# Two norms by halves of the tokens, later turns in an attention, and a short convolution in two parts, in a hybrid block with a two-layer mixer behind it

## Reference

```
def rms_norm_2(x, g):
    return x * rsqrt(mean(x * x, -1) + EPS) * g
for l in range(2):
    hx = modulate(rms_norm_2(x, norm1_g[l]), mod_x[0], mod_x[1])
    x = x + mod_x[2] * token_mixers(...)          # conv of 31 taps, differential attention, spatial gating, 3-tap conv, then @ w_out
    x = x + mod_x[5] * (square(relu(modulate(rms_norm_2(x, norm2_g[l]), mod_x[3], mod_x[4]) @ w1[l])) @ w2[l])
return rms_norm_2(x, final_g)

# first layer's attention, one head, one block of 128 queries
s = where(valid, q @ k.T * Dh**-0.5, NEG);  p = exp(s - max(s));  o = (p @ v) / sum(p)
# 3-tap convolution of the mixer
y_d = bg * depthwise_conv(cg * xin, conv_d_w)
```

## Time and profile before

| | |
|---|---|
| Runs | 2136.23, 2140.30, 2147.45 us; median 2140.3 |
| Profiled execution | 2144.59 us, its span 2142.8 us, 26206 instructions |
| Busy share of the span | TensorE matmul 96%, weight load 81%, VectorE 59%, ScalarE 37%, GpSimd 4% |
| Mean granted clock of TensorE | 0.990 of full speed |
| HBM | read 232.53 MB, written 12.06 MB |

### The profile page before, as it was taken

The page is one execution under the profiler, slowest core; times in us unless marked ns, Lnnn a source line. Parts: engine busy times, 40 slices in busy tenths (PEclk is TensorE's granted clock), DMA queues, the critical chain, the costliest instruction groups (busy, mean ns, idle before and its releaser), DMA issues.

```text
span 2142.8 us, 26206 instructions
## 1 busy us (share of the span) xinstructions
PE 2050.4 (96%) x11020; PEld 1740.1 (81%) x11020; DVE 1267.6 (59%) x1674; ACT 792.9 (37%) x1107; POOL 75.1 (4%) x83
## 2 busy tenths in 40 slices
PE   6999999999999999899999999999998899999998
PEld 5978877878788988788888888888787787888886
DVE  6466765766756886736546456464689645343343
ACT  4333334495253355524212122122536634232231
POOL 0000000000030000021000000001100010000001
PEclk9999999999999999999999999999999999999999
DMA  8543432523422531213323233232353122222221
GB/s 288 219 149 127 177 118 93 196 91 121 194 84 94 165 99 50 69 59 120 109 98 118 92 127 116 99 119 89 128 165 89 70 89 79 98 99 99 98 97 61
DMA packets 53077, 249.17 MB, mean 116 GB/s; under 512 B 6272, under 2 KB 10512, under 8 KB 34528
## 3 DMA queue, kind: packets, MB, share of 16 engines
q1 hardware_dynamic: 51072, 242.41, 32.8%
q10 hardware_dynamic: 1296, 2.63, 0.3%
q0 software_dynamic: 592, 2.46, 0.3%
HBM read 232.53 MB, written 12.06 MB: 114 GB/s over the span
## 4 chain that ended last, share of the span: by engine, by line
PE 82%; DVE 10%; ACT 3%; issue 3%; DMA 1%; POOL 0%; ACTq 0%; DVEq 0%; SPq 0%; POOLq 0%
PE banks L1805 68%; DVE small L1313 2%; ACT whi_f L1955 1%; DVE wlo_f L2146 1%; PE banks L631 1%; DMA mvr<-in_mst 1%; PE banks L622 1%; PE banks L1828 1%; PE banks L1830 1%; PE banks L1829 1%; PE banks L511 1%; DVE ntx L2180 1%; PE banks L586 1%; PE banks L585 1%; PE banks L587 1%
## 5 line engine op out<-in xcount | busy, mean ns | idle before, releaser
L1805 PE MATMUL banks<-hxh,whi_f 128*128 128x512 f32 x1440 | 583.9, 405 | 23.6 <-ACT hxh L1966 10.0
L1805 PE MATMUL banks<-hxh,wlo_f 128*128 128x512 f32 x1440 | 568.3, 395 | 0.0
L1805 PE MATMUL banks<-hxl,whi_f 128*128 128x512 f32 x1440 | 554.1, 393 | 0.0
L2146 DVE TENSOR_TENSOR wlo_f<-raw_f,whi_f 128x2048 fp32r<-128x2048 f32 x133 | 305.0, 2293 | 184.9 <-ACT whi_f L1955 184.8
L1955 ACT ACTIVATE whi_f<-raw_f 128x2048 fp32r<-128x2048 f32 x133 | 253.7, 1908 | 309.1 <-PE banks L1805 290.9
L1805 PEld LDWEIGHTS banks<-hxh,whi_f 128*128 128x128 f32 x1440 | 273.2, 190 | 87.0 <-issue 28.4
L1805 PEld LDWEIGHTS banks<-hxh,wlo_f 128*128 128x128 f32 x1440 | 272.9, 190 | 60.3
L1805 PEld LDWEIGHTS banks<-hxl,whi_f 128*128 128x128 f32 x1440 | 272.5, 189 | 58.7 <-issue 1.9
L1457 DVE SCALAR_TENSOR_TENSOR xT<-banks,small,xT 128x512 f32<-128x512 f32 x80 | 59.5, 750 | 253.2 <-PE banks L1805 253.2
L1805 PE MATMUL banks<-fxh,whi_f 128*128 128x512 f32 x512 | 202.8, 396 | 2.2 <-DVE cT L1457 1.1
L1805 PE MATMUL banks<-fxh,wlo_f 128*128 128x512 f32 x512 | 201.0, 393 | 0.0
(11 more groups left out here) (329 smaller groups left out, 3127.8 us busy)
## 6 DMA issues: line engine op xcount, KB each, us to landing
raw_f<-in_wst SPq DMA_DIRECT2D x133, 1024.0 KB, 4.8
mvr<-in_mst SPq DMA_DIRECT2D x120, 512.0 KB, 5.7
stack<-qk_parts SPq DMA_DIRECT2D x36, 192.0 KB, 6.7
x_kept<-xT SPq DMA_DIRECT2D x2, 2048.0 KB, 8.5
raw_f<-in_wst SPq DMA_DIRECT2D x8, 384.0 KB, 5.9
xT<-x_kept SPq DMA_DIRECT2D x2, 1536.0 KB, 8.7
qk_parts<-qk_h SPq DMA_DIRECT2D x3, 768.0 KB, 3.8
qk_parts<-qk_l SPq DMA_DIRECT2D x3, 768.0 KB, 3.6
```

Source lines behind the costliest of these rows:

```text
L1805: last = pe.matmul(o, (wh, wl)[w][:, k, c, :], r[part][:, k, :], start=(k == order[0] and parts is not LOW and (w, part) == (0, 0)), stop= ...
L2146: dve.tensor_tensor(wlo[r][:], raw[r][:], whi[n % 2 if n > N_FIRST else n][:].bitcast(F32), ALU.subtract).then_inc(w_lo, 1)
```

## The change

First attention: turned and values move from 9 and 12 steps behind the scores to 11 and 15. Short convolution: its six operations are put behind the maxima of two consecutive units, three and three; the low part of the first output chunk and `sub_norm(0)` come one unit later each. Layer 1's last output chunk and its last feed-forward chunk are multiplied by halves h of the tokens (256 columns each): both c of the first half, then both of the second, with sums, root, inverse and spread of the first half's norm inside the second. The first feed-forward chunk behind it takes pieces: four tiles of the first half, four tiles of the second half, then four whole tiles. The final products and the stores go by halves too, in five stores instead of eight. Cut to its core (the list of semaphore counts and the ScalarE and VectorE halves of the same steps are left out):

```diff
 def unit_turned(u):
-    return unit_scores(u) + 9
+    return unit_scores(u) + 11
 
 
 def unit_values(u):
-    return unit_scores(u) + 12
+    return unit_scores(u) + 15
...
+PIECES = [(h, k) for h in range(2) for k in range(4)] + [(None, k) for k in range(4, KT)]
+def columns(h):
+    return slice(0, T) if h is None else slice(TH * h, TH * h + TH)
...
-                gemm(n, 1, own)
-                norm_sums(SX, n_ff[l], nsq2)
-                norm_spread(SX, n_ff[l])
-                gemm(n + 1, 0, own, ready=(lambda k: wait_high(SX, n_ff[l], k), lambda k: wait_low(SX, n_ff[l], k)))
+                half_gemm(n, hxh, hxl, n_ff[1], nsq2)
+                piece_gemm(n + 1, n_ff[1], nsq2)
...
+                        if l and n == base + N_FF - 1:
+                            half_gemm(n, fxh, fxl, n_fin, nsqf)
+                            half_sums(n_fin, nsqf, 1)
+                            half_spread(n_fin, 1)
+                            continue
...
-            norm_root(SX, n_ff[l])
-            for k in range(KT):
-                norm_high(SX, n_ff[l], hxh, k, mod_shift(1, k, 0))
+                    half_square(n_ff[1], nsq2, c, 0, n)
+                half_root(n_ff[1], 0)
+                half_square(n_ff[1], nsq2, 0, 1, n)
+                for i, (_, k) in enumerate(PIECES):
+                    if i == 2:
+                        half_square(n_ff[1], nsq2, 1, 1, n)
+                    if i == 4:
+                        half_root(n_ff[1], 1)
+                    piece_high(n_ff[1], i, mod_shift(1, k, 0))
             split(n + 2)
...
-            run(p.cut, p.units, late={p.cut: short_conv, p.cut + 1: lambda: split(base + N_WIN),
-                                         p.cut + 2: lambda: sub_norm(0)})
+            run(p.cut, p.units, late={p.cut: lambda: short_conv(0), p.cut + 1: lambda: short_conv(1),
+                                         p.cut + 2: lambda: split(base + N_WIN), p.cut + 3: lambda: sub_norm(0)})
...
             else:
+                q = n_ff[1]
                 for c in range(2):
-                    last_x(c)
-            norm_inverse(SX, n_ff[l])
-            modulate(SX, n_ff[l], xT, hxh, hxl, 1, 0)
+                    half_residual(q, n, 0, c, 0)
+                half_inverse(q, 0)
+                half_residual(q, n, 0, 0, 1)
+                for i in range(len(PIECES) + 1):
+                    if i == 2:
+                        half_residual(q, n, 0, 1, 1)
+                    if i == 4:
+                        piece_low(q, 3)
+                        half_inverse(q, 1)
+                    if i < len(PIECES):
+                        piece_scale(q, i)
+                    if i > 0 and i != 4:
+                        piece_low(q, i - 1)
             split(n + 2)
...
+                    if end and not two and i == 3:
+                        for c in range(2):
+                            half_residual(n_fin, n, 1, c, 0)
+                        half_inverse(n_fin, 0)
+                        half_residual(n_fin, n, 1, 0, 1)
+                        continue
...
+            def final(k, h):
+                x_ = xT[:, k, columns(h)]
+                dve.scalar_tensor_tensor(x_, x_, vcol("final_g", k, 1), aux[:, 1 + h, 0:TH], ALU.mult, ALU.mult
+                                         ).then_inc(x_done, 1)
+            dve.wait_ge(SX.spread, half_count(n_fin, 0))
+            for k in range(KT):
+                if k == 5:
+                    half_residual(n_fin, base + N_FF - 1, 1, 1, 1)
+                final(k, 0)
+            half_inverse(n_fin, 1)
+            dve.wait_ge(SX.spread, half_count(n_fin, 1))
+            for k in range(KT):
+                final(k, 1)
...
-            for k in range(KT):
-                sync.wait_ge(x_done, KT + k + 1)
-                sync.dma_start(out[:, k, :], xT[:, k, :]).then_inc(stored, 16)
-            sync.wait_ge(stored, 16 * KT)
+            stores = [(0, 0, 4), (0, 4, 8), (1, 0, 4), (1, 4, 6), (1, 6, 8)]
+            for h, k0, k1 in stores:
+                sync.wait_ge(x_done, KT * (1 + h) + k1)
+                sync.dma_start(out[:, k0:k1, columns(h)], xT[:, k0:k1, columns(h)]).then_inc(stored, 16)
...
+            def half_sums(q, sq, h):
+                if h:
+                    pe.wait_ge(SX.rooted, half_count(q, 0))
+                else:
+                    pe.wait_ge(SX.added, q.a + KT - 3)
+                for i, slot in enumerate((0, KT - 2, KT - 1)):
+                    if i:
+                        pe.wait_ge(SX.squared, q.s + KT - 2 + 2 * h + i)
+                    for j in (2 * h, 2 * h + 1):
+                        last = pe.matmul(SX.st[:, j:j + 1], sq[:, slot, j * P:(j + 1) * P], ones[:, 0:1],
+                                         start=(i == 0 and j == 2 * h), stop=(i == 2), skip_group_check=True)
+                last.then_inc(SX.summed, 1)
+            def half_spread(q, h):
+                pe.wait_ge(SX.inverted, half_count(q, h))
+                for j in range(2):
+                    last = pe.matmul(aux[:, 1 + h, j * P:(j + 1) * P], SX.rs[:, 2 * h + j:2 * h + j + 1].to_broadcast([P, P]),
+                                     ident, start=True, stop=True)
+                last.then_inc(SX.spread, 1)
+            def half_gemm(n, hi, lo, q, sq):
+                weights(n)
+                for h in range(2):
+                    r = [(hi[:, :, columns(h)], lo[:, :, columns(h)])]
+                    for c in range(2):
+                        if h == 0:
+                            pe.wait_ge(acc_free[c], n)
+                        for k in range(KT):
+                            if (h, c, k) == (1, 0, 4):
+                                half_sums(q, sq, 0)
+                            if (h, c, k) == (1, 1, 1):
+                                half_spread(q, 0)
+                            last = step(n, n % 2, k, c, r, at=lambda r: acc[:, c, T * h:T * h + TH])
+                        last.then_inc(acc_ready[c] if h else x_part, 1)
+            def piece_gemm(n, q, sq):
+                weights(n)
+                for i, (h, k) in enumerate(PIECES):
+                    if i == 2:
+                        half_sums(q, sq, 1)
+                    if i == 4:
+                        half_spread(q, 1)
+                    r = [(hxh[:, :, columns(h)], hxl[:, :, columns(h)])]
+                    wait_high(SX, q, i)
+                    for c, parts in ((0, HIGH), (1, HIGH), (0, LOW), (1, LOW)) if k < KT - 1 else \
+                            ((0, HIGH), (0, LOW), (1, HIGH), (1, LOW)):
+                        if i == 0 and parts is HIGH:
+                            pe.wait_ge(acc_free[c], n)
+                        if c == 0 and parts is LOW:
+                            wait_low(SX, q, i)
+                        last = step(n, n % 2, k, c, r, (0 if i == 0 else -1, KT - 1),
+                                    lambda r: acc[:, c, columns(h)], parts, True)
+                        if k == KT - 1 and parts is LOW:
+                            last.then_inc(acc_ready[c], 1)
```

153 lines of the change are left out of this document (109 added, 44 removed).

## The result

The changed kernel took 2117.36 us (median of 4 runs, 2115.37 to 2123.61), the kernel before in the same comparison 2141.52 (4 runs): ratio 0.9891, 95% interval 0.9857 to 0.9926. The forecast was 2116.5. A second comparison of the same kernel (experiment 10) gave 2120.13 against 2144.69, 0.9881 (0.9859 to 0.9904). The medians differ by 24.2 and 24.6 us, 1.1 to 1.2%.

What follows compares the result with a forecast made beforehand. TensorE, 82% of the chain, was taken as the bound, with the gain in its waits and half-clock stretches. Terms -11.5 - 1.7 - 6.8 - 1.8 - 2.1 = -23.9 us from the median 2140.3 gave 2116.5, range 2108 to 2127.

Steps and rivals of the forecast that it cites:

- First attention, -11.5 and -1.7: First attention: TensorE's waits for turn and values go from 15.1 to 3.6 us; a half-clock stretch near 343 ends.
- one step more before the values, so 1.76 - 0.69 = 1.07: First attention: the fifth unit's copy moves behind a chunk end, leaving TensorE a new 1.07 us wait before the values.
- Convolution, -6.8: Second block's attentions: splitting the convolution shortens TensorE's turn waits in both layers and ends half clock behind them, -6.8 us.
- Layer 1's 1.4: Layer 1's convolution: of 2.0 us moved away only 1.4 counts, since the combination must await its own exponentials.
- without a wait over 0.5: Expected sign: the turns at 876.7 and 1706.2 us, behind the convolution, come without a wait over 0.5 us.
- Layer 0's 2.6: Layer 0's convolution: moving three operations a unit later takes 2.6 us from TensorE's 2.86 us wait.
- The join, -1.8: Chunk before layer 1's second norm, by halves: chunk 2.1 us longer, next-but-one chunk starts 17.0 behind its end; -1.8 us.
- The end, -2.1: Final chunk, norm and products by halves: chunk 2.1 us longer, then 6.4 instead of 10.6 to the last product; -2.1 us.
- (1): Rival: first attention's waits move instead of ending, as later copies fall behind chunk ends; half the gain lost, 2123; chance 0.17.
- (2): Rival: join by halves is no gain, TensorE's idle before late weight halves brings 1.2 GHz; 2122 to 2125.5; chance 0.15.
- (3): Rival: the split convolution brings no more than its later place costs, +6.8 us, 2123; chance 0.05.
- (4): Rival, slower: weight loads bind in the 240 new narrow matmuls, each 0.19 us more, +45.6, 2162; chance 0.02.

Runs made afterwards that it cites:

- experiment 10: The changed kernel unedited, measured again in a second comparison with the kernel before: 2120.13 us against 2144.69, ratio 0.9881.
- experiment 9: Changed kernel with scaled output ahead of the next exponential, weights' high part earlier, high-part products first, later steps for first attention's last waits: 2109.76 us, ratio 0.9833.
- Experiments 7, 8 and 12: On the changed kernel: 7 moves the weights' high part before the join's fifth piece (join 51.76 us); 8 multiplies high-part products first (2112.23 us); 12 both (2115.06 us).
- experiment 6: Changed kernel with last chunk, final norm and stores whole again, the join still by halves: 2124.27 us, one run.
- experiment 1: Kernel before with only the first attention's steps changed (9 and 12 become 11 and 15): 2127.71 us against 2145.78, ratio 0.992.
- experiment 3: Kernel before with only the three-tap convolution split in two parts: layer 1's stretch from gating's sums to transposes 50.00 us.
- experiment 2: Kernel before with only the first attention's values moved to 15 steps, the turn left at 9: first attention's stretch 339.7 us, 9.4 less than before.

## Why the prediction was right, and where its steps were not

**The total** came out at 2117.4 for 2116.5 (by its own sum, 2140.3 - 23.9, it is 2116.4). That it came so close is luck: the first attention was undersized by 4.2, and the others were oversized by 2.7 together by the table, by 4.1 by the means given above. The lower end of the range, 2108, isn't what it is said to be: the bounds of attention and convolution together give 2110.6.

**First attention, -11.5 and -1.7: right in place, too small.** Measured 17.4. Two steps failed. First, "one step more before the values, so 1.76 - 0.69 = 1.07": I counted what the new order puts between scores and turn (the values of the unit before), not what it puts between a copy and its values, which is the next unit's scores. For the fifth unit these are the sixth's, from 167.5 to 168.7; so its wait vanished, and the thirteenth's was 0.65 instead of 1.8. The last unit's, forecast 0.7, was 0.91. Left 1.6 instead of 3.6: 2.0 of the 4.2. Second, a wait was priced at its idle time in the trace. Removing two waits of 0.91 and 0.65 in experiment 9 shortened the stretch by 1.8 to 1.9, some 0.15 more for each; ten waits fewer and one stretch at half clock (13.5 + 1.6) gave 17.4, 0.2 more for each. The turn behind a wait is itself recorded longer (0.87 to 0.88 us, mostly 0.82 without one). The Trainium skill's Perfetto Trace Analysis (Tensor Engine Instruction) says that TensorE's end time is estimated from the instruction's size, "a model, not a measurement"; the difference agrees in sign with idle that is read from such ends, but no run here shows that this is its cause.

**Convolution, -6.8: right in kind.** Measured 3.1 and 2.7. Layer 1's 1.4 is what the executions without half clock show. It leaves 0.8 of the 2.19 us wait, and 0.79 is what the turn at 1680.42 waits; the sign "without a wait over 0.5" contradicted the sum, and fell. Layer 0's 2.6, for which no row was given, was 1.5 to 2.1: the turn a unit later, at 859.06, now waits 0.55 us, a remainder that I took as none. The half clock at the wait was there in layer 0 in all three profiles with the convolution whole and ScalarE's order as before, in layer 1 in two of the three. So 1.4 for each was right in size (1.6 in layer 0, 1.3 in layer 1) and not certain in layer 1.

**The join, -1.8: mechanism right, size wrong.** All its events came: the chunk 2.4 us longer (forecast 2.1), the idle at the fifth piece, ScalarE's and then VectorE's weight half last, 17.5 behind the chunk's end (17.0). The failed terms are small ones of one sign. Sums and spread took 1.24 + 0.44 where 1.55 stood; the narrow matmuls took 0.121; VectorE's second run of pieces began 5.1 instead of 4.7 behind the chunk and its last low part ended 14.1 behind it, 0.9 later than I had added up; ScalarE's weight half began 13.2 behind it where 12.6 stood. The formula that the prediction sets beside its rows is given by the Trainium skill's TensorE page (TensorE: Matmul & The Clock Gate, Back-to-back issue gap) for an isolated matmul, and not for a stream with weight loads; the measured 0.121 us decides. Experiments 7, 8 and 12 show what the late weight half costs: 1.9 us of the join, more than the halves gain in any execution. The prediction had this wait in its sum.

What the sum did not see is that the join before has no one length: 6.8 or 10.2 us of half clock, by execution. Against the shorter one the halves bring nothing. So even the 0.9 is that of a profile with the longer stretch.

**The end, -2.1: 1.3.** The last chunk +2.4; from its end to the last product 6.1 us (forecast 6.4) instead of 10.5; but the tail to the end of the span, "taken as it is", grew from 2.7 to 3.4. That is the step that failed: the last store lands later, a median of 3.0 us behind its issue instead of 2.2 for the same 256 KB, and with the old stores (experiment 6) the tail is 2.65 again. The new stores have rows of 1 KB instead of 2 KB and stand behind stores of 512 KB; no run tells which of the two counts.

**The rivals.** (1) fell with experiment 1. (2) was half right: no gain at the join in some executions, but by the late weights, not by the clock. TensorE stands idle there 1.11 and 2.07 us, and the granted clock stayed 1.00 through it in all eight executions with the join by halves. It fell to 0.50 in all six with the join whole. In the kernel before it fell at 1770.3, behind 2.4 us in which TensorE did no more than sums (stretch, us, busy by engine, PEclk):

```profile
1767.90:1770.30 2.40, 1.68 (x15) 1.59 (x14) 0.72 (x1) 0.63 (x1) 0.00 (x0) 1.00 0.63 154
1770.40:1774.70 4.30, 2.08 (x8) 1.79 (x9) 1.67 (x4) 1.11 (x3) 0.00 (x0) 0.50 0.35 149
```

The Trainium skill's TensorE page (TensorE: Matmul & The Clock Gate, Part 1) says that idleness throttles the array. The join whole agrees with it; the two idles of the join by halves, 1.11 and 2.07 us, did not bring it about, so the rival that the rule favoured was the wrong one. (3) fell with experiment 3. (4) fell by the rows: fourteen starts of 256-wide matmuls from 1738.38 to 1739.94 are 0.120 apart.

## What to carry to other kernels

When an order on one engine is moved, list for each wait, not for one, what comes to stand between its producer and its consumer; and ask which engine's half stands last at a join, since the gain ends there. A long operation (here the convolution) often hurts only through one queue position: the place of two operations in ScalarE's order was worth 7.9 us by itself. Price a wait on TensorE a little above its recorded idle, and judge changes of 1 us by stretches between named instructions, with the half-clock stretches in them counted, not by one execution's total.

## What the runs showed of the hardware that was not expected

**Two paces at full clock.** A full feed-forward block of layer 0 is 762 matmuls in one piece of the chain, without a wait and at granted clock 1.00. In one execution (experiment 10):

```profile
1042.03 132.74 PE banks L1957 x762
...
1176.09 134.98 PE banks L1957 x762
...
1312.38 132.74 PE banks L1957 x762
```

Of 42 such blocks in 14 profiles 23 took 132.5 to 132.7 us and 19 took 134.7 to 135.0; within one block 240 matmuls take 41.6 or 42.4. Identical code showed both. Three such blocks are up to 6.8 us between two executions. The cause is open; no run was made for it.

**Half clock comes and goes by execution.** The changed kernel's two profiles have 3.4 us of it once and six times ahead of the end, at 1.4 to 1.6 us each where TensorE hardly waits. Behind waits of 1.98 and 2.46 us in the first attention there was a stretch once in three and three times in three executions of the same order; behind the 2.26 of experiment 2 none.
